# Attention tails: half of each output projection moved in among the last three units, and the units reordered

## What is computed

| attention | units | keys of a unit (blocks of 128) | shape of POOL's operation |
|---|---|---|---|
| NSA | 8 | qt=0: 2 x 1, qt=1: 2 x 2 | 128x128, 128x256 |
| DSA | 8 | qt=0: 2 x 1, qt=1: 2 x 2 | 128x128, 128x256 |
| MLA ctx, layer 0 | 4 | 2 | 128x256 |
| MLA x, layers 0 and 1 | 4 each | 4 | 128x512 |

## Time and profile before

### The profile page before, as it was taken

The page is one execution under the profiler, slowest core; times in us unless marked ns, Lnnn a source line. Parts: engine busy times, 40 slices in busy tenths (PEclk is TensorE's granted clock), DMA queues, the critical chain, the costliest instruction groups (busy, mean ns, idle before and its releaser), DMA issues.

```text
span 1842.1 us, 22406 instructions
## 1 busy us (share of the span) xinstructions
PE 1614.7 (88%) x9499; PEld 1166.8 (63%) x9499; DVE 714.0 (39%) x1633; ACT 325.1 (18%) x774; POOL 79.9 (4%) x92
## 2 busy tenths in 40 slices
PE   6998999999998999999788987799998698876565
PEld 4774778888765788888667766645444485732122
DVE  2223367777235388775342243201204414310002
ACT  3032310000215100001231222211001323200000
POOL 0001300000005000000010020000000002000000
PEclk8986999999999999999899997699999799888888
DMA  9637469886842666784442325099997332579997
GB/s 362 209 132 247 162 244 357 320 320 224 263 136 93 228 227 215 289 315 149 136 147 83 137 92 228 28 410 408 409 409 282 115 138 92 228 289 409 409 409 284
DMA packets 168535, 443.69 MB, mean 241 GB/s; under 512 B 7754, under 2 KB 21236, under 8 KB 168436
## 3 DMA queue, kind: packets, MB, share of 16 engines
q1 hardware_dynamic: 168068, 442.13, 64.5%
q10 hardware_dynamic: 368, 0.13, 0.0%
HBM read 441.20 MB, written 1.05 MB: 240 GB/s over the span
## 4 chain that ended last, share of the span: by engine, by line
PE 67%; DMA 9%; DVE 7%; issue 3%; ACT 2%; POOL 2%; PEld 1%; PEldq 0%; ACTq 0%; SPq 0%; DVEq 0%
PE bank L647 65%; DMA ring<-in_w_gate 3%; DMA ring<-in_w_up 3%; POOL scr L1830 2%; PE bank L658 2%; DMA scr<-in_w_gate 1%; DMA scr<-in_w_up 1%; DMA ring<-in_w_down 1%; DVE scr L1878 1%; PEld bank L647 1%; DVE scr L1886 1%; DVE xT L2403 1%; DVE scr L2278 0%; DVE ctxT L2403 0%; DVE scr L2363 0%
## 5 line engine op out<-in xcount | busy, mean ns | idle before, releaser
L647 PE MATMUL bank<-hT,ring 128*128 128x256 f32 (+1 forms) x2576 | 514.5, 390 | 22.6 <-ACT hT L1511 21.0
L647 PEld LDWEIGHTS bank<-hT,ring 128*128 128x128 f32 (+1 forms) x2576 | 418.7, 182 | 115.8 <-issue 37.7
L647 PE MATMUL bank<-scr,ring 128*128 128x256 f32 (+3 forms) x1604 | 351.9, 380 | 14.4 <-DVEq L2246 5.8
L647 PEld LDWEIGHTS bank<-scr,ring 128*128 128x128 f32 (+2 forms) x1604 | 291.0, 190 | 65.0 <-issue 17.6
L1944 DVE SCALAR_TENSOR_TENSOR scr<-scr,csil 128x512 f32<-128x512 f32 x420 | 291.0, 749 | 3.2
L647 PE MATMUL bank<-scr 128*32 128x512 f32 (+8 forms) x1760 | 254.0, 469 | 39.3 <-DMA scr<-in_w_up 9.8
L647 PE MATMUL bank<-ring,scr 128*32 128x512 f32 (+2 forms) x1664 | 209.1, 618 | 50.2 <-DMA ring<-in_w_up 19.7
L647 PEld LDWEIGHTS bank<-scr 128*32 128x32 f32 (+4 forms) x1760 | 150.7, 160 | 140.3 <-issue 83.4
L647 PEld LDWEIGHTS bank<-ring,scr 128*32 128x32 f32 (+2 forms) x1664 | 69.3, 117 | 181.2 <-issue 112.9
L1830 POOL TENSOR_SCALAR scr<-scr,small 128x256 f32<-128x256 f32 (+2 forms) x88 | 79.7, 925 | 1476.3 <-DVE small L1994 1300.1
L2411 DVE TENSOR_TENSOR brow<-brow,bank 128x512 f32<-128x512 f32 x12 | 7.9, 686 | 255.4 <-ACT brow L1798 255.4
(11 more groups left out here) (229 smaller groups left out, 993.2 us busy)
## 6 DMA issues: line engine op xcount, KB each, us to landing
ring<-in_w_gate SPq DMA_DIRECT2D x24, 2048.0 KB, 22.9
ring<-in_w_down SPq DMA_DIRECT2D x24, 2048.0 KB, 23.5
scr<-in_w_ada SPq DMA_DIRECT2D x23, 2048.0 KB, 8.8
ring<-in_w_up SPq DMA_DIRECT2D x18, 2048.0 KB, 23.6
scr<-in_l_mod_w SPq DMA_DIRECT2D x14, 2048.0 KB, 16.0
scr<-in_w_up SPq DMA_DIRECT2D x14, 2048.0 KB, 20.8
ring<-in_l_mod_w SPq DMA_DIRECT2D x10, 2048.0 KB, 9.8
ring<-in_l_ffn_wg SPq DMA_DIRECT2D x10, 2048.0 KB, 13.7
```

Source lines behind the costliest of these rows:

```text
L647: ins = nc.tensor.matmul(out, lhsT, rhs, start=start, stop=stop, skip_group_check=True)
```

## The change

The four parts, and the diff cut to its core:

1. In every attention, `first_half` does the 32 matmuls of the projection's first half at three places: rows 0 to 3 for output columns 0 to 511 (16 matmuls, banks 4 and 5) at step N, between the transposes of unit N-2 and V of unit N-3; rows 0 and 1 for columns 512 to 1023 (8 matmuls, banks 6 and 7) at step N+1, after V of unit N-2; rows 2 and 3 (8) at step N+2, after V of unit N-1. `out_proj` keeps the second half.
2. NSA does its long units first and the short ones last.
3. DSA goes short, long, long, short, long, short, long, short; the first half waits for the first four units' results.
4. `k1` is projected into a bank of DVE's and copied by DVE.

```
-            return [(qt, c) for qt in range(NT) for c in range(4)]
+            return [(qt, c) for qt in (1, 0) for c in range(4)]
 def dsa_units():
-            return [(qt, cp) for qt in range(NT) for cp in range(4)]
+            return [(0, 0), (1, 0), (1, 1), (0, 1), (1, 2), (0, 2), (1, 3), (0, 3)]
...
+            def first_half(w, y, pair, rows):
+                for k in rows:
+                    for c in range(4 * pair, 4 * pair + 4):
+                        mm(banks[4 + c // 2][:, (c % 2) * T:(c % 2 + 1) * T], w[:, k, c * P:(c + 1) * P], y[:, k, :],
+                           start=k == 0 and c % 2 == 0, stop=False)
-            def out_proj(keys, y, sq=None):
-                w = use(keys[0]).rearrange("p (c n) -> p c n", c=4)
-                for k in range(4):
-                    accumulate(w[:, k, :], y[:, k, :], k == 0)
-                release()
-                w = use(keys[1]).rearrange("p (c n) -> p c n", c=4)
+            def out_proj(key, y, sq=None):
+                w = use(key).rearrange("p (c n) -> p c n", c=4)
                 finish([(w[:, k, :], y[:, 4 + k, :]) for k in range(4)], sq)
...
-            def attention(N, S, V, n_blocks, pt_, pr_):
+            def attention(N, S, V, n_blocks, pt_, pr_, out_key, units_needed=0):
...
+                    if i == N:
+                        pe.wait_ge(exp_done, 2 * (u0 + N - 1))
+                        if units_needed:
+                            pe.wait_ge(mixed_copied, u0 + units_needed)
+                        w = use(out_key).rearrange("p (c n) -> p c n", c=4)
+                        first_half(w, yT, 0, range(4))
                     if i >= 3:
...
                         V(i - 3, banks[u % 2], pt_[:, u % 2])
+                    if i == N + 1:
+                        pe.wait_ge(exp_done, 2 * (u0 + N))
+                        first_half(w, yT, 1, range(2))
+                    if i == N + 2:
+                        first_half(w, yT, 1, range(2, 4))
+                        release()
...
-            b = bank_for_act()
-            to_T(b[:, 0:T], w, 0, P, signal=pe_to_act)
+            b = bank_for_dve()
+            to_T(b[:, 0:T], w, 0, P, signal=pe_to_dve)
...
-            attention(len(units1), S1, V1, lambda i: 2 * (units1[i][0] + 1), pt1, pr1)
+            attention(len(units1), S1, V1, lambda i: 2 * (units1[i][0] + 1), pt1, pr1, ("out", 1, 0), 4)
...
-            b = job()
-            nc.scalar.copy(k1, b[:, 0:T]).then_inc(act_read, 1)
...
+            b = job()
+            nc.vector.tensor_copy(k1, b[:, 0:T]).then_inc(dve_read, 1)
```

More of the change, by code:

```diff
@@ L910, in ffn @@
                 settle()
-            def attention(N, S, V, n_blocks, pt_, pr_):
+            def attention(N, S, V, n_blocks, pt_, pr_, out_key, units_needed=0):
                 u0 = n["unit"]
+                assert u0 % 2 == 0 and N % 2 == 0
                 pe.wait_ge(dve_read, n["dve"])
@@ L1089, in _ @@
             ada_pieces(ADA_AT["lru"])
-            attention(len(units), S, V, lambda i: 2 * (units[i][0] + 1), pt, pr)
+            attention(len(units), S, V, lambda i: 2 * (units[i][0] + 1), pt, pr, ("out", 0, 0))
             mixed()
-            out_proj([("out", 0, 0), ("out", 0, 1)], yT, hT)
+            out_proj(("out", 0, 1), yT, hT)
             settle()
@@ L1154, in V1 @@
                                signal=mixed_done if last and s and g else None)
-            attention(len(units1), S1, V1, lambda i: 2 * (units1[i][0] + 1), pt1, pr1)
+            attention(len(units1), S1, V1, lambda i: 2 * (units1[i][0] + 1), pt1, pr1, ("out", 1, 0), 4)
             mixed()
-            out_proj([("out", 1, 0), ("out", 1, 1)], yT, hT)
+            out_proj(("out", 1, 1), yT, hT)
             settle()
@@ L1317, in mixers @@
                 release()
-                attention(len(units2), S2, V2, lambda i: nk // P, pt2, pr2)
+                attention(len(units2), S2, V2, lambda i: nk // P, pt2, pr2, ("out2", layer, 0))
                 mixed()
-                out_proj([("out2", layer, 0), ("out2", layer, 1)], yT)
+                out_proj(("out2", layer, 1), yT)
                 settle()
```

## The result

The changed kernel takes 1834.24 us, the median of six runs (1828.87 to 1834.69); the kernel before, run beside it, 1843.83 (1841.97 to 1847.85). The ratio is 0.9948 [0.9931, 0.9964]. The forecast was 1834.3. The profiled execution has a span of 1832.9 us against 1842.1.

What follows compares the result with a forecast made beforehand. TensorE bounds nearly everywhere, POOL holds NSA and DSA's second part. From 1843.93 us, 3.8 (NSA) + 1.5 (k1) + 2.4 (DSA) + 1.3 (ctx) + 1.6 (MLA x) - 0.6 (waits) = 10.0; forecast 1834.3, eight in ten 1829 to 1840.5.

Steps and rivals of the forecast that it cites:

- The case in which the 68 us vanish: All five attentions: the moved matmuls' whole time disappears, 1776 us; given under 1%.
- NSA, 3.8 forecast: NSA with long units first: gain 4.0 us from its shorter tail, 3.8 with handovers off.
- the extra 0.9 + 0.35: NSA's start: long units delay POOL by 0.9 us of first scores and 0.35 of DVE and ACT work.
- A: Each attention's tail: end of the transposes of unit N-2, where moved matmuls may begin; 197.05 us in NSA.
- DSA, 2.4 forecast: DSA in alternating order: projection at 591.4 against 593.98 gives 2.6 us, 2.4 after handovers.
- ctx and MLA x: MLA tails: filled TensorE idle time gains 1.3 us in ctx and 0.8 in MLA x, twice.
- The 0.64 of nothing: MLA x's tail: TensorE's rows nearly end to end until 1096.54, then 0.64 us idle ahead of the projection.
- 0.6 us for about twenty of them: All attentions: new semaphore waits, met when reached, about four in each, cost 0.6 us in all.
- The slower case: NSA: TensorE stays at 1.2 GHz throughout; outweighs the gain beyond 204 us, about 1851 at 35 us; 4%.
- rival 1: NSA and DSA: reordering gives nothing, long units starve POOL under half clock; 5.8 us gain, 1838 to 1840; 17%.
- The transfers: MoEs: a rival had DMA set their end and gains ahead given back, 1842 to 1845; 7%.
- Rival 4: Whole kernel: filled tails keep the clock full at following norms and small waits fall in, 1826 to 1829; 6%.

Runs made afterwards that it cites:

- e1: The kernel before with only the k1 projection moved to a bank and copy of DVE's: 1839.04 us, ratio 0.9988.
- e5: The changed kernel unaltered, run once more on another chip: 1834.26 us, ratio 0.9957.
- e3: The changed kernel with NSA's units back in the old order, short ones first: 1831.96 us, ratio 0.9941.
- e6: The changed kernel with the half's first 16 matmuls ahead of the transposes of unit N-2, repeated on another chip: 1827.93 us, ratio 0.9922.
- e4: The changed kernel with the half's first 16 matmuls put ahead of the transposes of unit N-2: 1825.84 us, ratio 0.9922.
- e2: The kernel before with both new unit orders and the k1 move, the first half left behind the attention: 1842.49 us, ratio 0.9996.

## Why the prediction was right

**What is hidden.** The step that mattered most was that no moved matmul is free: only idle time that it fills counts. Leaving the half out took 61 us off; the change took 9.6. The case in which the 68 us vanish is refuted.

**NSA, 3.8 forecast, 3.02 found.** Step by step, each counted from the first score. POOL's start, +4.70 for +4.75: right, the extra 0.9 + 0.35 included. The half begins at 195.14 - 167.89 = 27.25 us; the forecast had A at 197.05 - 170.20 = 26.85. The 0.40 is mostly POOL's: its gaps are 0.56, of which I allowed 0.3, and its three rows sum to 24.08 us where I had 23.81. Each V of a short unit, three times, takes 0.95 (203.68 to 204.63), not 0.84: 0.33 more. I had scaled a long unit's 1.40 by records, 12 of 20, and it did not scale so. And the projection, which I took for the same length in pieces as in one, is not: from 195.14 to its end at 229.37 it is 34.23 us, less three V and the transposes (0.59) leaves 30.8, against 30.47. The forecast's raw 4.0 becomes 3.0 with these, and 3.02 was measured. The sizes were off, the mechanism was not.

**DSA, 2.4 forecast, 1.83 found.** The timelines of POOL and TensorE:

```profile
560.61 10.82 POOL L1846 TENSOR_SCALAR scr<-scr,small 128x128 f32<-128x128 f32 x14 [363.38 <-DVE small L2010]
571.75 1.18 POOL L1846 TENSOR_SCALAR scr<-scr,small 128x128 f32<-128x128 f32 x2 [0.32 <-DVE small L2010]
573.33 11.96 POOL L1846 TENSOR_SCALAR scr<-scr,small 128x256 f32<-128x256 f32 x16 [0.41 <-DVE small L2010]
```

```profile
583.03 0.66 PE L658 MATMUL bank<-tab,scr 128*128 128x128 f32 x4 [1.14 <-POOL scr L1846]
583.52 7.07 PE L647 MATMUL bank<-scr,ring 128*128 128x256 f32 x32
```

POOL's gaps, the cost of a long unit behind a short one, are 0.32 + 0.41 = 0.73, where I took 0.4. The first half begins 583.52 - 557.78 = 25.74 after the first score; forecast 588.8 - 563.3 = 25.5. A short V, 0.59 in this timeline and not 0.49, twice, is another 0.2. From 2.6 that leaves 2.2. The last 0.3 is the projection in pieces again: 7.00 us for the first 16 matmuls (to 590.52), 3.65 for the next 8 and 20.14 for the rest make 30.8, against 30.47 in one piece.

**ctx and MLA x.** 1.46 for 1.3, and 1.08 for 0.8 each. The 0.64 of nothing ahead of the projection was in my sum; what I had too high was the waits. I charged 0.6 us for about twenty of them that are met when reached. In the chain of the changed kernel the records of the tails follow each other with none between, and these three stages came out 0.7 above their terms, not below. Here the projection got shorter in pieces: in MLA x it is 33.87 us from 1082.14 to 1116.02, and three V (1.79 each) and the transposes (0.87) leave 27.6, against 27.88 in one piece; in ctx it is 27.65. Why the pieces cost 0.3 in NSA and DSA and save 0.25 in each MLA stage is open. A term for waits was not needed.

**k1.** 1.7 for 1.5; e1, with this part alone, shows the same.

**The clock.** The windows of NSA in the changed kernel, against the earlier trace rows:

```profile
176.00:180.00 4.00, 3.74 (x15) 2.59 (x16) 3.45 (x15) 2.22 (x9) 4.00 (x6) 0.50 1.05 388
180.00:184.00 4.00, 4.00 (x40) 3.09 (x39) 2.94 (x16) 2.67 (x10) 4.00 (x5) 0.79 1.05 402
184.00:188.00 4.00, 4.00 (x46) 2.92 (x43) 3.75 (x23) 2.94 (x12) 4.00 (x6) 1.00 1.02 399
```

The long units ran with 1.2 GHz until after 180 and with 2.4 from 184, as short ones did before, and POOL stayed at 4.00 of 4.00 us under either. NSA had 10.2 us of half clock here, 13.0 in e5 (the same kernel) and 13.2 before. The slower case, half clock to beyond 204, did not come; neither did the part of rival 1 in which long units starve POOL. By the rule cited from the Trainium skill, TensorE: Matmul & The Clock Gate, Part 4, long units with twice the transposes could have held the clock down; the trace does not bear that out here, and no run isolates it. Over the eleven profiled executions NSA had from 3.0 to 17.1 us of half clock, 17.1 with the short units first, in e3.

**The transfers.** Ahead of the two MoEs the DMA stands still as before, in the windows' last two columns:

```profile
1132.00:1142.00 10.00, 3.20 (x19) 2.67 (x17) 7.59 (x24) 3.87 (x7) 0.00 (x0) 0.67 0.00 1
1595.00:1608.00 13.00, 6.72 (x33) 6.19 (x34) 7.90 (x25) 3.98 (x7) 0.00 (x0) 0.63 0.01 2
```

So the stream restarts at TensorE's release and passes the gain on. The stretches with the MoEs, between the two MLA x stages and behind the second, are 0.4 us longer each than before (413.26 for 412.82, 253.22 for 252.80), so about that much at most was given back at either.

**How far the agreement goes.** 1834.3 against 1834.24 is closer than the working deserves, and that much of it is luck. The terms are off by up to 0.8 us each and cancel, the ratio's interval allows any gain from 6.6 to 12.7 us, and single executions of the changed kernel lie 6 us apart in the first series and 12 in the second. What the range had to hold was this scatter and the terms' errors, and it did. Rival 4 deserves a note: the rest of the tail's idle time was there to be had, but only with the piece one place earlier, a choice that I did not question in the diff.

## What to carry to other kernels

Moving work into a pipeline's tail saves the idle time there and no more: count from the point where the moved work may start to the point where the next stage started, subtract what must be done between them, and let the moved work drop out. Then ask whether its place could be one wait earlier, for that wait is idle time too: here it brought about 2.5 us more in NSA and DSA, where the whole change had brought 4.85. Find the engine that paces the pipeline by its busy time in a window of that stage, not by its share of the program (POOL is busy 4% of the span and 98% of NSA's 176 to 192 us), and before you move its work to another engine look how full that one is in the same window.

## What the runs showed of the hardware

The same code took different times in single executions, by where the clock was at half. The stretch ahead of NSA, in no kernel changed, took from 167.5 to 175.0 us over the eleven profiled executions, with 37.5 to 54.6 us at half clock. One block in the projections of ctx, 184 records, took 39.32 us in the changed kernel and 36.41 in e6. The windows of just this block in the one and in the other:

```profile
885.76:925.08 39.32, 39.32 (x184) 32.96 (x185) 8.55 (x14) 6.25 (x12) 0.00 (x0) 0.92 0.30 107
```

```profile
883.65:920.06 36.41, 36.41 (x184) 30.81 (x185) 8.54 (x14) 6.25 (x12) 0.00 (x0) 1.00 0.32 116
```

TensorE is busy all the time in both; the one has a stretch at 1.2 GHz inside, and pays 2.9 us. DVE and ACT did the same work in the same time. Totals fall into groups that go with the clock: the six runs of e4 are 1824.95 to 1826.20 four times, with a mean granted clock of 0.938 to 0.941, and 1833.69 and 1833.82 twice, with 0.936. A change of a few microseconds here is read from the lengths of its stages first, and from totals only over many runs. The lengths are not free of the clock either. POOL's timeline in DSA of e6, whose kernel is that of e4 and whose clock was at half for 10.2 us of the stage and not 3.4:

```profile
570.26 1.19 POOL L1846 TENSOR_SCALAR scr<-scr,small 128x128 f32<-128x128 f32 x2 [0.69 <-DVE small L2010]
572.50 11.99 POOL L1846 TENSOR_SCALAR scr<-scr,small 128x256 f32<-128x256 f32 x16 [1.04 <-DVE small L2010]
```

POOL's two gaps grew from 0.72 to 1.73 us in all, and the stage with them from 57.68 to 58.69. So in NSA and DSA a difference of up to about 1 us between two single executions counts only where their clocks are alike. In MLA the lengths of kernels with the same code agree within 0.02 us, and those stages had no half clock in any execution. What decides in which of these groups an execution falls, and whether an edit can shift it, no run here settles; the missing 2.8 us of e2, the 3.7 of e3 and what is left of e6's 3.5 may all be of this kind, or not.
